# Expert results to their tokens: from indirect scatters and pair loads to one-hot matmuls, two experts in one product

## The reference, cut to what matters

```python
hg = jnp.einsum('nd,edf->nef', t, w_gate)          # 16 experts, 1024 -> 512
hu = jnp.einsum('nd,edf->nef', t, w_up)
act = jax.nn.silu(hg) * hu * gates[..., None]      # gates: two of 16 are not zero
x = x + jnp.einsum('nef,efd->nd', act, w_down)     # 512 -> 1024, summed over experts
...
gate = jax.nn.sigmoid((rmsnorm(x, norm_ple_w) @ w_ple_gate))
x = x + gate * (p @ w_ple_proj)
y = rmsnorm(x, final_norm_w)
```

## Time and profile before

| | us |
|---|---|
| median of 3 runs (lowest, highest) | 716.59 (714.49, 718.78) |
| the profiled execution, its own time | 713.99 |
| its span, first to last instruction | 712.2 |
| PE busy | 641.1 (90%) |
| DVE, ACT, POOL busy | 304.4, 179.6, 84.5 |
| mean granted TensorE clock | 0.956 of full speed |

### The profile page before, as it was taken

One profiled execution on the slowest core, in us unless ns is written; L12 is line 12 of the kernel. 1 busy time (PEld: TensorE's weight loads), 2 busy tenths in 40 slices (PEclk: granted clock), 3 DMA queues, 4 the chain that ended last, 5 costly groups with the idle time before them and its releaser, 6 DMA issues. The chain is left out here.

```text
span 712.2 us, 8297 instructions
## 1 busy us (share of the span) xinstructions
PE 641.1 (90%) x3187; PEld 435.7 (61%) x3187; DVE 304.4 (43%) x881; ACT 179.6 (25%) x426; POOL 84.5 (12%) x103
## 2 busy tenths in 40 slices
PE   3899999899979999999999759999889797798996
PEld 2688888786678987888877523333333232233785
DVE  0368377865497999853200570101000010015543
ACT  3222338413432222534200511111001010100323
POOL 5000024210011111100000010212111111101000
PEclk9999999999997999999999959999999899999799
DMA  9733358996143563617896726999999999998101
GB/s 250 251 118 119 119 182 270 347 348 219 30 121 108 187 214 113 208 30 236 352 393 258 296 98 243 378 422 423 424 423 424 423 422 421 423 378 305 56 1 61
DMA packets 45346, 179.72 MB, mean 252 GB/s; under 512 B 3933, under 2 KB 12577, under 8 KB 36976
## 3 DMA queue, kind: packets, MB, share of 16 engines
q1 hardware_dynamic: 34704, 147.21, 53.0%
q0 software_dynamic: 10080, 30.80, 13.7%
q10 hardware_dynamic: 520, 1.15, 0.4%
HBM read 167.65 MB, written 17.65 MB: 260 GB/s over the span
## 5 line engine op out<-in xcount | busy, mean ns | idle before, releaser
L851 PE MATMUL bank<-hT,arena 128*128 128x264 f32 x832 | 194.1, 394 | 5.3 <-DVE hT L1702 3.1
L851 PEld LDWEIGHTS bank<-hT,arena 128*128 128x128 f32 x832 | 159.6, 194 | 33.8 <-DMA arena<-in_w_in 3.5
L1250 PE MATMUL bank<-arena,hT 128*64 128x512 f32 x512 | 123.2, 635 | 22.3 <-DMA arena<-in_w_exp_up 16.5
L1250 PEld LDWEIGHTS bank<-arena,hT 128*64 128x64 f32 x512 | 40.8, 146 | 96.3 <-issue 95.0
L1702 DVE SCALAR_TENSOR_TENSOR hT<-hT,arena,bank 128x256 f32<-128x256 f32 x16 | 7.7, 480 | 155.5 <-ACT hT L1614 155.5
L1694 DVE TENSOR_TENSOR arena<-arena 128x256 f32<-128x256 f32 (+8 forms) x140 | 57.1, 456 | 21.5 <-ACT arena L1507 10.5
L1072 PE MATMUL bank<-arena 128*128 128x264 f32 x256 | 58.3, 387 | 2.6 <-issue 1.3
L1282 PE MATMUL bank<-arena,sq 128*64 128x512 f32 x256 | 58.5, 598 | 1.4 <-ACT sq L1619 1.4
L1072 PEld LDWEIGHTS bank<-arena 128*128 128x128 f32 x256 | 48.3, 190 | 11.9 <-issue 2.1
L1439 ACT ACTIVATE arena<-bank 128x264 f32<-128x264 f32 x44 | 17.0, 388 | 137.9 <-PE bank L851 137.9
L1614 ACT ACTIVATE hT<-bank 128x256 f32<-128x256 f32 x16 | 6.1, 383 | 145.6 <-PE bank L1250 145.6
(11 more groups left out here) (263 smaller groups left out, 688.5 us busy)
## 6 DMA issues: line engine op xcount, KB each, us to landing
arena<-in_w_exp_gate SPq DMA_DIRECT2D x16, 2048.0 KB, 25.5
arena<-in_w_exp_up SPq DMA_DIRECT2D x16, 2048.0 KB, 29.9
arena<-in_w_exp_down SPq DMA_DIRECT2D x16, 2048.0 KB, 23.1
arena<-in_w_in SPq DMA_DIRECT2D x13, 2048.0 KB, 10.6
out<-arena POOLq DMA_DIRECT2D x18, 512.0 KB, 4.5
arena<-in_w_out SPq DMA_DIRECT2D x4, 2048.0 KB, 8.6
arena<-in_state_ssm POOLq DMA_DIRECT2D x8, 512.0 KB, 8.0
arena<-in_state_hgrn POOLq DMA_DIRECT2D x8, 512.0 KB, 4.8
```

Source lines behind the costliest of these rows:

```text
L851: last = mm(ps[:, 0:T], w[:, k, j * P:(j + 1) * P], hT[:, k], start=(k == 0), stop=(k == KT - 1))
L1250: last = mm(bank[p][r, :].rearrange("p (w f) -> p w f", w=2), xgT[:, p, k % 4, CAP * (k // 4):CAP * (k // 4) + CAP], gu[:, :, k, FF // 2 * ...
```

## The change

All 16 experts now take the way of one-hot matmuls, two experts in one product. Expert 2j puts its first half on partitions 0 to 63, expert 2j + 1 on 64 to 127 (its down product writes the two halves the other way round), so that `ys[:, half]` holds 64 tokens of each of two experts on 128 partitions. `hot[:, half]` is the one-hot matrix of these 128 rows against 264 tokens. One pair is 8 `mm` calls of 128x128 by 264 columns (`add_pair`) and 8 DVE adds to `xT` (`pair_add`).

Pairs 0 to 5 (`IN_LOOP`) are added inside `halves_gate_up` of t = 3, 5, ..., 13: ahead of each of its 8 steps k one `mm` call of pair (t - 3) / 2. They use banks 4 and 7 in turn; the first call of a pair waits for the copies of expert t - 2, for `hot`, and for ACT's `ple_take` of the job just before, since bank 4 is shared. Pair 6 comes after GU(15), pair 7 at the end. D(14) moves behind GU(15). `halves_result` is two copies of 64 partitions instead of one of 128. DVE makes the `hot` of a pair in four instructions of 64 partitions. The scatters, the pair loads, their adds and transposes remain in the overflow branch alone; gathers have POOL's queue to themselves, and SP issues the weights of the per-layer gate after GU(14).

```diff
@@ block.sync
-            eng.wait_ge(main.gu_full, SENT)
-            for p in range(2):
-                eng.wait_ge(main.sent[p], 16 * (SENT // 2))
-            for k in range(TOP_K):
-                r = pair_rows[k * T:(k + 1) * T]
-                eng.dma_start(pairs[:, 0:2, k], ...).then_inc(pair_in, 16)
-                eng.dma_start(pairs[0:NS, 2, k], r[NP_:T]).then_inc(pair_in, 16)
             eng.wait_ge(main.gu_full, E - 1)
             ple_gate_weights(ld_pg)
@@ block.gpsimd
-            def scatter_halves(t):
...
                     gather_halves(t)
-                    if 3 <= t < SENT + 3:
-                        scatter_halves(t - 3)
...
-            eng.tensor_tensor(pairs[:, 0, 0], pairs[:, 0, 0], pairs[:, 0, 1], ALU.add).then_inc(acc_ready, 1)
@@ block.tensor
+            def add_pair(j, m):
+                n = KT * j + m
+                half, k = m // 4, m % 4
+                if m % 4 == 0:
+                    eng.wait_ge(main.d_took, 4 * j + (4 if j < IN_LOOP else 3 + half))
+                    eng.wait_ge(hot_ready, 4 * j + 2 + 2 * half)
+                if n > 1:
+                    eng.wait_ge(sum_took, sum_free(n))
+                if j < IN_LOOP:
+                    eng.wait_ge(ple_took, min(2 * j + 2, PLE_JOBS))
+                mm(sum_bank(n)[:, 0:T], ys[:, half, k * P:(k + 1) * P], hot[:, half], start=True, stop=True
+                   ).then_inc(sum_full, 1)
@@ halves_gate_up
                 for k in range(KT):
+                    if t % 2 and 3 <= t < E - 1:
+                        add_pair((t - 3) // 2, k)
                     for c in range(2):
@@ halves_down
+                        half = c if t % 2 == 0 else 1 - c
+                        r = slice(CAP * half, CAP * half + CAP)
@@ the tail of the loop
             halves_gate_up(E - 1)
-            add_late(E - 2, 0)
+            for m in range(KT):
+                add_pair(PAIRS - 2, m)
             halves_act(E - 1)
+            halves_down(E - 2)
             halves_down(E - 1)
-            add_pairs(KT)
-            add_late(E - 1, 2 * KT)
+            for m in range(KT):
+                add_pair(PAIRS - 1, m)
@@ block.vector
             def halves_result(t):
                 p = t % 2
                 eng.wait_ge(main.d_full, t + 1)
-                if t >= 2:
-                    eng.wait_ge(main.sent[p], t // 2 * 16)
-                nc.vector.tensor_copy(ys[:, p], bank[6 + p][:, :]).then_inc(main.d_took, 1)
+                for half in range(2):
+                    r = slice(CAP * (half ^ p), CAP * (half ^ p) + CAP)
+                    nc.vector.tensor_copy(ys[r, half], bank[6 + p][r, :]).then_inc(main.d_took, 1)
+            def turn(t):
+                summed = t % 2 and t >= 3
+                if summed:
+                    pair_add((t - 3) // 2)
                 halves_mul(t)
                 halves_result(t - 1)
+                if summed:
+                    hot_tokens((t - 1) // 2)
...
+            halves_mul(E - 1)
+            pair_add(PAIRS - 2)
+            hot_tokens(PAIRS - 1)
             halves_result(E - 2)
-            ...
             halves_result(E - 1)
+            pair_add(PAIRS - 1, weigh)
```

More of the change, by code:

```diff
@@ L795, in _ @@
                     eng.wait_ge(over.sent[p], 16 * E)
[L796 to L799, removed]
-            eng.tensor_tensor(pairs[:, 0, 0], pairs[:, 0, 0], pairs[:, 0, 1], ALU.add).then_inc(acc_ready, 1)
+                eng.wait_ge(pair_in, 64)
+                eng.tensor_tensor(pairs[:, 0, 0], pairs[:, 0, 0], pairs[:, 0, 1], ALU.add).then_inc(acc_ready, 1)
+            move_tokens(CHECK + 3, E)
         @block.tensor
@@ L826, in norm_part @@
                 eng.wait_ge(sq_done, k * KT + c + 1)
-                last = mm(ps[:, 0:T], ones, sq[:, c] if k < 2 else sq_end[:, LATE_ORDER[c] if k == 2 else c], start=(c == 0), stop=(c == KT - 1))
+                last = mm(ps[:, 0:T], ones, sq[:, c] if k < 2 else sq_end[:, c], start=(c == 0), stop=(c == KT - 1))
                 if c == KT - 1:
@@ L1300, in ple_job, with add_over @@
                 last.then_inc(ple_full, 1)
[L1302 to L1319, removed]
+            def add_over():
                 eng.wait_ge(acc_ready, 3)
                 for ft in range(KT):
-                    ps = open_sum(first + ft)
+                    if ft >= 4:
+                        eng.wait_ge(o_sum_took, ft - 3)
+                    ps = SUM_BANK[ft % 4]
                     for i, (t0, n) in enumerate(TOK):
                         last = nc.tensor.transpose(ps[:, t0:t0 + n], pairs[0:n, i, 0, ft * P:(ft + 1) * P], ident[0:n, 0:n])
-                    last.then_inc(sum_full, 1)
+                    last.then_inc(o_sum_full, 1)
+                eng.wait_ge(o_sum_took, KT)
             eng.wait_ge(a_took, ja["ht", 2, 1] + 1)
@@ L2171, in sum_add, with hot_tokens @@
[L2171 to L2175, removed]
+                for half in range(2):
+                    r = slice(CAP * (half ^ p), CAP * (half ^ p) + CAP)
+                    nc.vector.tensor_copy(ys[r, half], bank[6 + p][r, :]).then_inc(main.d_took, 1)
+            def hot_tokens(j):
+                for half in range(2):
+                    for low in range(2):
+                        r = slice(CAP * low, CAP * low + CAP)
+                        t = 2 * j + (half ^ low)
+                        ts(hot[r, half], K[r, K_IOTA:K_IOTA + T], -1.0, ALU.add, slot_at[r, t:t + 1], ALU.is_equal
+                           ).then_inc(hot_ready, 1)
@@ new lines, in pair_add, with over_add @@
+            def pair_add(j, then=lambda m: None):
+                for m in range(KT):
+                    n = KT * j + m
+                    eng.wait_ge(sum_full, n + 1)
+                    tt(xT[:, m], xT[:, m], sum_bank(n)[:, 0:T], ALU.add).then_inc(sum_took, 1)
+                    if m:
+                        then(m - 1)
+                then(KT - 1)
+            def over_add():
+                eng.wait_ge(pair_in, 64)
+                for i in range(1, 3):
+                    n = TOK[i][1]
+                    tt(pairs[0:n, i, 0], pairs[0:n, i, 0], pairs[0:n, i, 1], ALU.add).then_inc(acc_ready, 1)
+                for ft in range(KT):
+                    eng.wait_ge(o_sum_full, ft + 1)
+                    tt(xT[:, ft], xT[:, ft], SUM_BANK[ft % 4][:, 0:T], ALU.add).then_inc(o_sum_took, 1)
```

103 lines of the change are left out of this document (43 added, 60 removed).

## The result

The kernel after takes 730.85 us (median of 4 runs, 729.07 to 734.31), the kernel before, run beside it, 716.28 (4 runs, 714.49 to 718.78): ratio 1.0207, 95% interval 1.0153 to 1.0261. It is slower, as forecast, but by 14.6 us where 7.5 were worked out, and just outside the range. Its profiled execution took 729.07 us with a span of 727.3; the forecast for the profiled execution was 721.5.

A forecast was written before the change was run, and what follows sets the result against it. Weight transfers bound the loop; with pair products PE would: 612.8 + 36.3 + 2.75 puts GU(15) at 651.9, plus a 19.75 us tail the last adds come 7.5 us later, 716.59 + 7.5 = 724.1 us; range 709 to 730.

The forecast's parts named there:

- The step that failed: PE's own loop time: turn 11's transposes over D(11) and the branch to GU(12) 8.45 us, turn 12 without its wait 12.0.
- The rival that touched it: Branch at expert 12 gets cheap as the DMA empties: about 7.2 us less, 716.9 us; chance 0.17 with partial cases.
- Small terms: In the loop: a pair costs 6.05 us of PE, and five waits for ACT's ple copy 2.75 us together.
- The alternation: Odd GU turns: each step k pays 0.355 us for changing tile shape there and back, 2.5 us a pair.
- the first rival: Alternating shapes in the loop cost nothing, a pair 3.56 us, total 709.1 us; chance 0.15.
- The third rival: A pair in the loop costs 7.5 us, or waits at each call hold PE's stream: 732.8 us; chance 0.08.
- The loop bound by PE: Expert loop turns from waiting for weights to waiting for PE, GU(15) at 651.9 us, 18 us over the transfers' floor.
- The scatters' DMA time: Removing 14 scatters frees 4.4 us of DMA time, 4.1 ahead of the last up weights, worth nothing once PE binds.
- The transfers' floor for GU(15): Earliest GU(15) that weight transfers allow without the scatters: 633.4 us.
- The tail: From GU(15) to the first of the last adds: 24.45 us before, 19.75 after, 4.7 us won.

The follow-up runs named there:

- after, `add_over` left out: Kernel after without the 24 transposes that the change put into PE's overflow part: 724.88 us, ratio 1.0129.
- after, `add_over` four times: Kernel after with the same 24 transposes standing four times in PE's overflow part: 724.05 us, ratio 1.0117.
- after, short jump: Kernel after with PE's overflow part cut to one wait, so PE still jumps but over next to nothing: 722.87 us, ratio 1.0101.
- after, turned round: Kernel after, on PE alone the usual path falls through at expert 12, a copy of the rest stands behind the overflow part: 723.15 us, ratio 1.0106.
- after, calls in a run: Kernel after with a pair's 8 calls in a run ahead of GU, in four banks, instead of one ahead of each step: 715.32 us.
- run behind GU: Kernel after with a pair's 8 calls in a run behind GU(t), four banks, DVE's adds behind the gate's multiplication: 713.89 us, ratio to before 0.997.
- run behind GU, turned round: Kernel after with each pair's calls in a run behind GU and PE's usual path falling through at expert 12: 704.43 us, ratio to before 0.9872.

## Why the prediction was right and wrong

The stretch at expert 12 in the programs of this case, in us. "Gaps" are PE's idle times ahead of the pieces of GU(12); the last column is GU(15)'s start after GU(1)'s.

| PE's program | D(11)'s end to GU(12)'s end | gaps | GU(15) |
|---|---|---|---|
| before | 14.3 | 3.82, 1.12 | 205.6 |
| after | 20.3 | 5.65, 2.14 | 225.8 |
| after, `add_over` left out | 12.2 | 3.45 | 217.6 |
| after, `add_over` four times | 14.3 | 4.70 | 219.8 |
| after, short jump | 6.8 | none | 212.2 |
| after, turned round | 6.8 | none | 212.3 |
| after, calls in a run | 16.6 | 3.75, 2.92 | 207.4 |
| run behind GU | 17.6 | 4.31, 1.91 | 203.8 |
| run behind GU, turned round | 6.8 | none | 198.0 |

**The step that failed** is "from there over D(11) and the branch to GU(12) 8.45 (to 594.48), turn 12 without its wait 12.0": the branch's stretch was carried over from before unchanged, and took 10.3 (603.74 to 614.02) and 16.2 (to 630.18), 6.0 us more. The rival that touched it looked in the other direction only, a cheaper branch; so nothing of the range above the forecast stood for it. The mechanism of the forecast, a loop that turns from weights to PE, held, and it is what made this term count: in before the jump is covered by waits for weights. The row that could have warned is the earlier trace rows: a place with unexplained idle time, inside the stretch that becomes critical, in code that the change itself edits. Where the jump costs what it did in before (the kernel with `add_over` four times, 14.3 us), GU(15) stands at 219.8 us after GU(1); the forecast had 217.9 (651.9 less GU(1) at 434.0).

How the 6.0 us divide is shown by the windows of the kernel after: time, busy time of PE, PEld, DVE, ACT and POOL, granted clock, DMA share, GB/s.

```profile
606.00:608.00 2.00, 2.00 (x12) 0.57 (x8) 0.74 (x3) 0.00 (x0) 0.00 (x0) 1.00 1.02 410
...
610.00:612.00 2.00, 0.00 (x0) 0.00 (x0) 0.00 (x0) 0.00 (x0) 0.00 (x0) 0.92 1.06 422
612.00:614.00 2.00, 0.00 (x0) 0.01 (x1) 0.00 (x0) 0.00 (x0) 0.00 (x0) 0.50 0.93 389
...
622.00:624.00 2.00, 2.00 (x6) 0.47 (x4) 0.00 (x0) 0.00 (x0) 0.00 (x0) 0.50 1.00 422
...
626.00:628.00 2.00, 2.00 (x11) 0.69 (x8) 0.00 (x0) 0.00 (x0) 0.00 (x0) 1.00 0.16 66
```

PE is idle, the granted clock falls to 0.50 (1.2 of 2.4 GHz), and the instructions of GU(12) then run at half speed, 6 in a window instead of 12. Idle time grew by 2.85 us over before (7.79 against 4.94), and the two pieces of GU(12) took 12.6 us instead of 7.04, 5.6 of slow running against 2.4. So about half of the 6.0 is the wait and half the clock that follows it.

The Trainium skill, Runtime: NRT & Kernel Launch, Instruction fetch mechanics, has engines read code in blocks of 16 KiB (256 instructions) ahead of use, and a taken branch to a block that isn't there wait for it. The trace agrees, with pieces of 16 KB that land 1.4 to 2.3 us before each gap's end, and with the free short jump and the free fall-through; these runs put the stop at 5.4 to 13.5 us with its clock.

**Small terms, 1.5 us together.** A pair cost 6.18 us instead of 6.05, 0.8 for six. The first pair of the loop waited 1.01 us for DVE's copies, which the prediction held to be done by then, and the four waits for ACT's copy were 0.6 each: 3.4 us of waits instead of 2.75. With the 6.0 of the branch that is 7.5 of the 7.7.

**What held.** The alternation: 2.45 us a pair against 2.5 forecast, from rows of other places; so the first rival, free changes, is out. The Trainium skill, TensorEngine Tiling (Array Packing), Key Properties, says that a change of tiling mode drains TensorE; the trace agrees, with these 2.45 us. The third rival, 7.5 us a pair, is out by the 6.18. The loop bound by PE: no wait for weights left, though the weights keep ahead only narrowly (DMA share 0.98 from 440 to 606 us, 1.00 in before from 440 to 600). The scatters' DMA time: 4.2 us where before is bound by it; after waits for no weights, so there it buys nothing. The transfers' floor for GU(15), 199.4 us after GU(1): 198.0 in the fastest version. The tail: 24.45 to 19.64 us, 4.8 gained against 4.7. (The full DMA slices of the earlier trace rows are 26 to 36, counted from 1, where the prediction has 25 to 36; nothing hangs on it.)

## What to carry to other kernels

When a change moves the limit from transfers to an engine, go once more through every idle time of that engine in the stretch: those that were covered now count in full, and they may change with the code itself. A usual path should fall through a branch and not jump over the rare one, if PE is the limit. Products of another tile shape belong in a run, not between the steps of another product.

## What the runs showed of the hardware

A jump on PE over a long part costs 5.4 to 13.5 us here (stretches of 12.2 to 20.3 us against 6.8), over one wait nothing, and turned round nothing; the same program pays the same price in each of two executions (20.3 and 20.7; 14.3 and 14.4 us), and 24 transposes less or 72 more in the part jumped over make it 6 to 8 us cheaper. PE's code comes in pieces of 16 KB over the DMA engines that also carry the weights: one alone took 1.1 us (before, at 591.71), two at once 2.0 each (after, at 609.67), and PE went on 1.4 to 2.3 us after the landing. With hardly any weights moving the stretch falls from 20.3 to 12.1 us. The longest first gaps, 5.65 and 5.75 us, are those of the two executions in which two pieces started at the same moment; what sets the others, 2.64 to 4.70, stays open. Going from two 64-wide tiles to one of 128 and back costs 0.35 us (2.45 / 7).
